# A third seven-product pair in the first half of the up projections, and an earlier scaling of four token chunks

## The reference, cut to what matters

```
def swiglu(x, w_in, w_out):
    gate, up = jnp.split(x @ w_in, 2, axis=-1)
    return (jax.nn.silu(gate) * up) @ w_out
```

## Time and profile before

| what | value |
|---|---|
| three runs | 3083.72, 3088.42 and 3088.19 us; median 3088.19 us |
| the profiled execution's own time | 3087.5 us |
| span of its instructions | 3085.9 us |
| TensorE busy with matmuls, with weight loads | 2980.1 us (97%), 2800.6 us (91%) |
| VectorE busy | 2234.5 us (72%) |
| ScalarE busy | 1391.6 us (45%) |
| GpSimd busy | 131.5 us (4%) |
| mean granted TensorE clock | 0.987 |

### The profile page before, as it was taken

How to read it: one execution, slowest core, us unless ns; L and a number is a source line. 1 busy time by engine, 2 the same in 40 slices (tenths; PEclk the granted TensorE clock), 3 DMA queues, 4 the chain that set the end, 5 groups by cost and what they waited for, 6 DMA issues and landing times.

```text
span 3085.9 us, 77779 instructions
## 1 busy us (share of the span) xinstructions
PE 2980.1 (97%) x32512; PEld 2800.6 (91%) x32512; DVE 2234.5 (72%) x3930; ACT 1391.6 (45%) x2573; POOL 131.5 (4%) x247
## 2 busy tenths in 40 slices
PE   8999999999999999997999998999999999999998
PEld 7998999999887999997997777999999888899997
DVE  6767795876666595976547886795876676787784
ACT  4223463553555562542336665552553232364461
POOL 0000000001232000000000000000000000000000
PEclk9999999999999999999999999999999999999999
DMA  3222223232444222231220000323232222223231
GB/s 134 93 94 85 83 94 105 90 114 86 131 137 121 83 96 103 83 117 59 69 77 12 22 22 16 100 96 103 83 117 69 91 83 91 78 100 113 76 116 58
DMA packets 104673, 270.09 MB, mean 88 GB/s; under 512 B 12802, under 2 KB 45954, under 8 KB 104146
## 3 DMA queue, kind: packets, MB, share of 16 engines
q1 hardware_dynamic: 91346, 228.54, 21.7%
q0 software_dynamic: 13056, 37.64, 3.5%
HBM read 247.61 MB, written 18.52 MB: 86 GB/s over the span
## 4 chain that ended last, share of the span: by engine, by line
PE 84%; DVE 9%; ACT 3%; DVEq 2%; issue 2%; DMA 0%; SPq 0%; ACTq 0%
PE ps L855 26%; PE ps L756 24%; PE ps L765 5%; PE ps L829 3%; PE ps L767 3%; PE ps L768 3%; PE ps L769 3%; PE ps L1316 3%; PE ps L766 2%; PE ps L1294 2%; PE ps L916 1%; DVE arena_r L2378 1%; PE ps L1326 1%; PE ps L981 1%; PE ps L1413 1%
## 5 line engine op out<-in xcount | busy, mean ns | idle before, releaser
L756 PE MATMUL ps<-arena_r 128*128 128x272 f32 x7080 | 984.7, 295 | 42.7 <-DVE arena_r L2371 15.5
L756 PEld LDWEIGHTS ps<-arena_r 128*128 128x128 f32 x7080 | 916.2, 191 | 88.8 <-issue 55.5
L855 PE MATMUL ps<-arena_r 128*128 128x272 f32 x3648 | 497.5, 288 | 5.1 <-ACT ps L1843 5.1
L855 PEld LDWEIGHTS ps<-arena_r 128*128 128x128 f32 x3648 | 474.0, 188 | 5.9 <-ACT ps L1843 5.9
L855 PE MATMUL ps<-hb_r,arena_r 128*128 128x272 f32 x2736 | 381.5, 289 | 0.0
L855 PEld LDWEIGHTS ps<-hb_r,arena_r 128*128 128x128 f32 x2736 | 358.2, 188 | 0.0
L765 PE MATMUL ps<-arena_r 128*128 128x480 f32 x660 | 251.4, 381 | 0.0
L1807 ACT ACTIVATE arena_r<-ring 128x512 fp32r<-128x512 f32 x336 | 207.9, 622 | 94.5 <-DVE ring L2497 67.1
L1738 ACT ACTIVATE arena_r<-ring 128x1408 fp32r<-128x1408 f32 (+1 forms) x72 | 96.8, 1345 | 303.7 <-PE ps L769 280.8
L2512 DVE TENSOR_TENSOR arena_r<-ring,arena_r 128x512 fp32r<-128x512 f32 x336 | 223.7, 684 | 4.2 <-ACT arena_r L1807 3.2
L2438 DVE TENSOR_TENSOR arena<-ps,rstd 128x544 f32<-128x544 f32 x60 | 43.5, 724 | 225.6 <-PE ps L769 225.6
(11 more groups left out here) (454 smaller groups left out, 4769.1 us busy)
## 6 DMA issues: line engine op xcount, KB each, us to landing
ring<-in_w_up SPq DMA_DIRECT2D x176, 512.0 KB, 3.4
ring<-in_w_mix SPq DMA_DIRECT2D x112, 512.0 KB, 3.2
ring<-in_w_down SPq DMA_DIRECT2D x64, 704.0 KB, 4.2
arena<-in_hg_s POOLq DMA_DIRECT2D x16, 512.0 KB, 3.5
out_hg_so<-arena POOLq DMA_DIRECT2D x16, 512.0 KB, 2.9
ring<-in_w_hgout SPq DMA_DIRECT2D x16, 512.0 KB, 3.3
arena<-in_cache_k SPq DMA_DIRECT2D x128, 64.0 KB, 1.8
arena<-in_cache_v POOLq DMA_DIRECT2D x128, 64.0 KB, 2.2
```

The costliest lines, as they stand in the source:

```text
L756: mm = pe.matmul(PS[:, 2 * a + hf, 0:HALF], part[:, ws], rhs[:, o:o + HALF], start=start and n == 0, stop=stop and n == 2)
L855: mm = pe.matmul(PS[:, bank, 0:HALF], w[:, ws], rhs[c], start=start and c == 0 and n == 0, stop=stop and c == HC - 1 and n == 2, skip_grou ...
```

## The change

Pair 2 of the first half becomes a seven-product pair in all four layers, which adds three forms to the half (67 for 64). The order of `form_sum` calls is completed by one call in pair 1. ScalarE scales chunks 0 to 3 before it takes the high part of chunk 7, and the wait for the mixer's stores goes with them. The temporary tile of the HGRN output additions moves to another place. The wait for the turned tiles moves from pair 3 to pair 2.

```diff
+        hg_turned = arena_t[:, ar.at:ar.at + NT]
         hg_vt, hg_vts = ar.take(NP_TOK), ar.take(P)
...
-        UP = ("PPPSSSSSSSS", "SSSSSSSSSSS")
+        UP = ("PPSSSSSSSSS", "SSSSSSSSSSS")
...
-                            if p == 3 and not s and k in (1, 2, 4, 6):
+                            if p == 2 and not s and k in (1, 2, 4, 6):
                                 pe.wait_ge(S("ff_tl"), 8 * layer + 4 + {1: 1, 2: 2, 4: 3, 6: 4}[k])
...
+            def scaled_chunks(layer, half):
+
+                for c in range(half * HC, (half + 1) * HC):
+                    last = act.activation(ff_scaled[:, c * NT:(c + 1) * NT], x3[:, c, :], ACT.Copy,
+                                          scale=vec3[:, V_FFN + layer, c:c + 1])
+                last.then_inc(S("ff_th"), 1)
+
             def after_mixer(layer, c):
 
+                if c == KC - 1:
+                    act.wait_ge(S("st_out"), stored(layer))
+                    scaled_chunks(layer, 0)
                 x_sem, x0 = x_ready(layer, "m")
                 act.wait_ge(S(x_sem), x0 + c + 1)
                 high("ff_", V_FFN + layer, x3, ff_hh, c)
...
                     def first_pair():
-                        act.wait_ge(S("st_out"), stored(layer))
-                        for c in range(KC):
-                            last = act.activation(ff_scaled[:, c * NT:(c + 1) * NT], x3[:, c, :], ACT.Copy,
-                                                  scale=vec3[:, V_FFN + layer, c:c + 1])
-                            if c % HC == HC - 1:
-                                last.then_inc(S("ff_th"), 1)
+                        scaled_chunks(layer, 1)
                         form_high(0)
                         form_high(1)
                         turned_high(0)
...
                         gated(p - 1)
                         if begin:
                             turned_low(0)
+                            form_sum(j + 5)
                         else:
                             ahead(j)
                         ahead(j + 1)
...
-                    dve.tensor_tensor(halves(hg_f), acc((0, 1, 3, 2)[m % 4]), halves(rstd[:, :]), ALU.mult)
+                    dve.tensor_tensor(halves(hg_turned), acc((0, 1, 3, 2)[m % 4]), halves(rstd[:, :]), ALU.mult)
                     dve.drain()
                     xm = X[:, m * NT:(m + 1) * NT]
-                    dve.tensor_tensor(xm, xm, hg_f, ALU.add).then_inc(S(L + "x"), 1)
+                    dve.tensor_tensor(xm, xm, hg_turned, ALU.add).then_inc(S(L + "x"), 1)
                     after_mixer(layer, m)
```

## The result

| | before | after |
|---|---|---|
| median | 3086.68 us of 6 runs | 3100.09 us of 6 runs (3096.65 to 3103.40) |
| profiled execution, its span | 3087.5, 3085.9 us | 3103.4, 3101.8 us |

The account below looks back on a forecast made before the run. TensorE was taken to bound the stage, with VectorE having next to no reserve. 4 x 2.0 + 2 x 0.05 = +8.1 us on the median 3088.2 gave 3096.3 us, range 3089 to 3099.5.

Parts of the forecast that it names:

- the three waits: TensorE waits for ScalarE's copies: 1.5 us at pair 2's k = 2, 1.55 at its k = 3, 0.4 in pair 3.
- the 0.78 us of a sum: Each of the four sums added to VectorE's list ahead of pair 2's gated(1) costs 0.78 us.
- the high part of chunk 7 unmoved in layer 0: Early scaling fits ScalarE's gap in layers 0 and 3; in 1 and 2 the high part comes 0.54 us later, costing 0.05.
- The saving of 1.48 us: Pair 2 on TensorE: 10.57 us with seven products against 12.05 plain, 1.48 us a layer, 5.9 us in four.
- rival 1: TensorE's saving arrives whole, copies in pair 2 being in time: 3082.3 us; chance 0.08.
- Waits 3.45 us, less 1.48: +2.0 us a layer: Pairs 2 and 3: TensorE's waits of 3.45 us a layer outweigh the 1.48 us saved, net +2.0 us a layer.
- The start of pair 2: TensorE begins pair 2 of layer 0 at 378.98 + 12.05 = 391.03 us and wants k = 2 at 394.05.
- The third wait: Pair 3, k = 2: copied(0) near 408.05 us behind VectorE's last sum, wanted at 407.66, a wait of 0.4 us.
- upper bound: VectorE's steps 1 to 2% longer than taken: +2.4 to +3 us a layer, 3098 to 3100 us.
- Rival 2: One of pair 2's two waits is absorbed, ScalarE or VectorE being earlier: 0 to +3.3 us, 3088 to 3091.5; chance 0.22.
- Rival 3: VectorE never catches up, its reserve only 0.2 us a pair, so waits recur in each pair: 3098 to 3100 us; chance 0.12.
- Rival 4: Early scaling does not fit; chunk 7's high part is late in layers 0 and 3 too: +0.4 us; no chance of its own.

Follow-up runs that it names:

- the changed order: Changed kernel with ScalarE's copied(0) of pair 2 ahead of form 8, and VectorE's gated(1) ahead of turned lows 2 and 3: 3099.41 us, ratio 1.0035.
- the early norm: Changed kernel with the norm's matmuls between the two products of the first pair and the root ahead of form 0: 3097.07 us, ratio 1.0025.
- the mended kernel: Changed kernel with norm matmuls inside the first pair and copied(0) first in pairs 2 and 3 and the second half's pair 0: 3096.91 us, ratio 1.0030.

## Why the prediction was right and wrong

By its own steps, each against the start of pair 1 in layer 0:

| step | predicted | measured |
|---|---|---|
| `gated(1)` starts | 396.86 - 378.98 = 17.88 | 396.17 - 378.26 = 17.91 |
| pair 2, k = 2 starts | 395.55 - 378.98 = 16.57 | 394.91 - 378.26 = 16.65 |
| pair 2, k = 3 starts | 398.60 - 378.98 = 19.62 | 397.91 - 378.26 = 19.65 |
| pair 3, k = 2 starts | 408.06 - 378.98 = 29.08 | 407.50 - 378.26 = 29.24 |
| waits shown on the copies | 5 + 14 = 19 | 17.2 |
| cost of the pair in a layer | +2.0 | +2.52, +2.48, +2.84, +2.85 |

**What held.** The places of the three waits, who is behind them, the 0.78 us of a sum (393.16 back to 392.38 in VectorE's timeline), the reciprocal tied to the root, and the high part of chunk 7 unmoved in layer 0, 0.17 us behind its addition. The saving of 1.48 us arrives and is eaten. The pairs from 4 on have no waits. The rule of the Trainium skill (Perfetto Trace Analysis, Identifying the Most-Contended Engine) to optimize the engine with the highest occupancy first, which stood beside rival 1, was not borne out: TensorE had 48 matmuls less and the kernel took longer.

**What failed: the step "Waits 3.45 us, less 1.48: +2.0 us a layer".** The mechanism was right; the term was sized 2.0 and measured 2.5 to 2.85. The waits shown are no measure of it: they came out smaller than forecast (17.2 us for 19) and the cost larger. By the steps from one product to the next, layer 0 loses 0.16 + 1.58 + 1.49 + 0.11 + 0.43 + 0.11 = 3.88 us up to the fourth product of pair 3, less 1.48 is 2.40. Against the prediction's own steps:

- *The start of pair 2.* I took 391.03 from the chain's row. In TensorE's own timeline pair 3 before started at 402.91, where the chain has 403.08; the difference of 0.17 us stands at the pair's start, not at its end. The arithmetic then gave 0.15 too little: the start of k = 3 in pair 3 was 407.45 before, 28.47 us after pair 1's start, and by my own numbers it would come at 408.06 + 1.51 - 378.98 = 30.59, +2.12.
- *The third wait and the restart.* The first block after a wait takes 1.62 us to the next (397.91 to 399.53, 407.50 to 409.12), not 1.51; the prediction ended each wait and went on at full pace. The first of these two is absorbed, since TensorE waits again in pair 3. There product k = 2 is released 29.24 us after pair 1, for 29.08 in the forecast, because VectorE's last sum and the form and copy behind it come 0.16 us later. With this and the second restart, 0.11, the measured 30.86 us to k = 3 (409.12 - 378.26) are accounted for: 2.12 + 0.16 + 0.11 = +2.39.
- *0.1 us more* over pairs 4 to 10, to the 2.5 of layers 0 and 1.
- *Single delays of 0.35 us on VectorE* in layers 2 and 3. In layer 3 the last sum ahead of form 8:

```profile
2740.87 0.69 DVE L2518 TENSOR_TENSOR arena_r<-arena,arena_r 128x512 fp32r<-128x512 f32 x1
2742.00 0.69 DVE L2503 TENSOR_TENSOR ring<-ring 128x512 f32<-128x512 f32 x1 [0.44 <-issue]
```

It comes 1.13 us after the low, where layer 0 has 0.78. TensorE waits 1.69 us for the copy there, not 1.34, and the layer is 0.36 us longer. In layer 2 the first sum of pair 3 has 0.51 us of the same kind. The kernel before has such a delay too, and there it cost nothing:

```profile
456.57 0.69 DVE L2497 TENSOR_TENSOR ring<-ring 128x512 f32<-128x512 f32 x1 [0.45 <-issue]
```

Its stage is 178.63 us in each layer. With the change VectorE is the engine that sets the pace, so each delay of its list goes through to the end.

These delays stand at fixed places of VectorE's list. The trace of the kernel before has nine of them, with 0.43 to 0.51 us of idle time and no engine named. Counted over VectorE's instructions in the trace, waits and branches included, they are numbers 1116, 2260, 2516, 2772, 2900, 3924, 4052, 4437 and 5247. The kernel with the early scaling alone, whose list on VectorE is as long, has its nine at the same numbers. The changed kernel has seven: 3668, 3797, 4052, 5119, 5375, 5759 and 5887; numbers 3797 and 5375 are the two sums above. The pair alone, the changed order, the early norm and the mended kernel have theirs at just these seven. From 2260 to 4052 all are whole multiples of 128 apart (3797 to within one), also in the two kernels with extra sums, where others are hit (2388, 3540, 3924; 2388, 3796, 3924, 4052). So what is delayed depends on how many instructions stand ahead of it, and that layers 0 and 1 went free was luck of the count. What happens at these places is not shown.

That was in sight in part: the prediction said that VectorE has next to no reserve, and its upper bound (+2.4 to +3 us a layer) held this case as 1 to 2% on VectorE's steps. The value taken should have been nearer to that bound.

**Range and chances.** 4 x 2.0 + 0.1 gave 8.1; 11.0 was measured (10.7 in the stage and 0.3 in the first pairs), and 3088.2 + 11.0 = 3099.2 us would have been inside the range. The rest up to the median (3100.1), and the 1.5 us by which the base itself came out lower in six runs, have no place in the profile's stage. The prediction had no term for that: its range came from the stage's terms alone. The chance of 0.65 for "slower" was well placed; the value inside it was too low.

**The rivals.** Rival 1 (the saving whole) needed `gated(1)` 1.6 us earlier than followed; it came 0.03 later. Rival 2 (one wait absorbed) likewise. Rival 3 gave the nearest time (3098 to 3100) for the wrong reason: the waits do not recur in pairs 4 to 10. Rival 4: in layers 0 and 3 the high part is not late. In layer 1 it came behind the scaling; chunk 7 started 5.34 us after the first pair (1055.96 to 1061.30) for 5.29 before, the 0.05 us that were forecast, but its first six matmuls then took 0.86 us and not 0.75: the restart again. The price is 0.16 us, not 0.05, in each of layers 1 and 2. The kernel before has the same step of 0.86 us in layer 0, behind the 0.32 us by which chunk 7 is late there, so the restart could have been priced from its trace.

**What stays open.** What delays VectorE by 0.35 us at those fixed places of its list. Whether 1 to 3 us of the difference outside the stage belong to the change. Why a wait of 2 us or more is followed by a fall of the clock in eight places and not in four others.

## What to carry to other kernels

Before trading TensorE's work for VectorE's, add up the other engine's list over just the stage in question, from the point that pins its start (here the root) to the last thing that TensorE needs; 28% idle over the span said nothing on it. If that list is the longer one, reordering within it only moves the wait, and merging two short waits into one long one can cost more than it saves. A dose test (a few idle sums put in) shows before the change is written whether there is a reserve: here 2.3 us, for a change that takes 4.6 (3.1 of sums and the 1.5 by which TensorE would be sooner).

## What was not expected of the hardware

- After a wait, even one of 0.27 us, TensorE's first block of 12 matmuls takes 0.11 us longer (1.62 for 1.51), at a granted clock of 1.00. In the first pair of layers 1 and 2, six matmuls behind a pause of 0.05 us took 0.86 us for 0.75.
- Longer waits amid dense matmuls can drop TensorE's clock from 2.4 to 1.2 GHz. Three experiments (the changed order, four sums more, the mended kernel) have one wait of 2.05 to 2.69 us in each layer: behind eight of the twelve the next blocks ran slow (3.09 us for 12 matmuls at a granted clock of 0.50), behind four (2.28, 2.28, 2.33, 2.69 us) they didn't. Once it also fell behind two waits of 1.84 and 1.42 us (the pair alone, layer 3). At the end of the stage a fall cost about 1.1 us in the mended kernel (99.32 us for pairs 2 to 10 with it and 98.24 without), and 0.6 and 0.2 us in layers 1 and 2 of the changed order, where a later wait went away in exchange. In the changed kernel, whose longest wait is 1.69 us, no block ran slow.
- A GpSimd addition of 128 x 512 float32 values took 1.29 to 2.40 us (1.29 to 1.44 for the three beside VectorE's reciprocal in layer 2) where VectorE takes 0.69, and made a VectorE instruction with two inputs beside it 0.9 to 1.1 us longer.
- VectorE loses about 0.35 us at fixed places of its list, most of them a multiple of 128 instructions apart: a step of 1.13 us for 0.78. With a reserve this costs nothing, without one it goes through to the end.
